# Shorter recurrence on TensorE, and two sequences' pages copied during the first layer

## What is computed

```python
for layer in range(2):                       # layer 0 is even, layer 1 is odd
    y = _even_mixer(x, ...) if layer == 0 else _odd_mixer(x, ...)
    x = _layernorm(ALPHA * x + y, ...)
    x = _layernorm(ALPHA * x + _moe(x, ...), ...)

# _odd_mixer: two mixers side by side, concatenated, one output projection
# C: RWKV-7, per head of 64, token by token:
    sa = einsum('bhvk,bhk->bhv', S, kk_t)
    S = S * w_t - sa[..., None] * (kk_t * a_t) + v_t[..., None] * k_t
    y_t = einsum('bhvk,bhk->bhv', S, r_t)
# D: latent attention; the sample group also reads 16 cached pages per sequence,
#    found through page_table (8 sequences x 16 pages)

# _moe: one router, 16 SwiGLU experts, each row goes to two of them
    he = silu(h @ w_gate[e]) * (h @ w_up[e]);  y += gate * (he @ w_down[e])
```

## Time and profile before

| | us |
|---|---|
| median of 3 runs | 1127.14 |
| lowest, highest | 1124.95, 1130.03 |
| the profiled execution | 1126.0 |
| its span, first to last instruction | 1124.2 |
| mean granted TensorE clock | 0.954 |

### The profile page before, as it was taken

One profiled execution on the slowest core, in us unless ns is written; L12 is line 12 of the kernel. 1 busy time (PEld: TensorE's weight loads), 2 busy tenths in 40 slices (PEclk: granted clock), 3 DMA queues, 4 the chain that ended last, 5 costly groups with the idle time before them and its releaser, 6 DMA issues.

```text
span 1124.2 us, 26894 instructions
## 1 busy us (share of the span) xinstructions
PE 1011.9 (90%) x11002; PEld 658.2 (59%) x11002; DVE 501.6 (45%) x1261; ACT 329.7 (29%) x889; POOL 129.8 (12%) x152
## 2 busy tenths in 40 slices
PE   9999996699998599999887789999999938999995
PEld 3687454466664367777666677655655525666641
DVE  1581134322222636497645663876523352222217
ACT  0102114133333224223333333264421132333321
POOL 0010000210000300000222220411000011100013
PEclk9999998699999799999899999899999968999997
DMA  9752205999996632122322224494443098999935
GB/s 316 300 86 75 98 38 210 335 348 371 379 409 227 206 150 76 38 91 74 92 78 72 78 77 141 135 366 169 170 177 150 26 349 270 381 369 371 402 118 203
DMA packets 80867, 225.41 MB, mean 201 GB/s; under 512 B 9424, under 2 KB 50432, under 8 KB 62432
## 3 DMA queue, kind: packets, MB, share of 16 engines
q1 hardware_dynamic: 65184, 153.29, 37.5%
q0 software_dynamic: 11968, 57.71, 15.5%
q10 hardware_dynamic: 3584, 12.58, 3.0%
HBM read 201.57 MB, written 40.86 MB: 216 GB/s over the span
## 4 chain that ended last, share of the span: by engine, by line
PE 83%; DVE 5%; DMA 5%; issue 4%; ACT 2%; POOL 0%; DVEq 0%; POOLq 0%; SPq 0%; ACTq 0%
PE bank L1367 16%; PE bank L1271 10%; PE bank L1558 9%; PE bank L1391 8%; PE bank L1466 6%; PE bank L1492 3%; PE bank L1660 3%; PE bank L1349 2%; PE bank L1529 2%; DMA work<-xkept,idx 1%; DMA xkept<-x 1%; PE bank L1971 1%; PE bank L1996 1%; PE bank L1282 1%; DMA work<-yrows,rowi 1%
## 5 line engine op out<-in xcount | busy, mean ns | idle before, releaser
L1271 PE MATMUL bank<-ring,cat 128*128 128x512 f32 x256 | 112.6, 594 | 1.3 <-ACT cat L2163 1.3
L1558 PE MATMUL bank<-xT,ring 128*128 128x288 f32 x448 | 110.9, 407 | 0.0
L1558 PEld LDWEIGHTS bank<-xT,ring 128*128 128x128 f32 x448 | 84.6, 190 | 23.8 <-issue 1.1
L1367 PE MATMUL bank<-ring,work 128*32 128x128 f32 (+1 forms) x1344 | 83.0, 318 | 1.7 <-DVE work L2620 1.7
L2630 DVE TENSOR_TENSOR work<-work,bank 128x192 f32<-128x192 f32 x32 | 11.3, 354 | 157.0 <-ACT work L2123 157.0
L1271 PEld LDWEIGHTS bank<-ring,cat 128*128 128x128 f32 x256 | 47.5, 190 | 57.2 <-issue 57.2
L2639 DVE COPY work<-bank 64x512 f32<-64x512 f32 x64 | 44.0, 688 | 67.2 <-PE bank L1391 66.7
L1367 PEld LDWEIGHTS bank<-ring,work 128*32 128x32 f32 (+1 forms) x1344 | 58.1, 122 | 25.1 <-issue 13.1
L1466 PE MATMUL bank<-xT,ring 128*128 128x288 f32 x256 | 63.1, 407 | 0.0
L2123 ACT ACTIVATE work<-bank 128x192 f32<-128x192 f32 x32 | 10.6, 331 | 163.0 <-PE bank L1367 163.0
L1466 PEld LDWEIGHTS bank<-xT,ring 128*128 128x128 f32 x256 | 48.3, 190 | 13.5 <-issue 0.4
(11 more groups left out here) (491 smaller groups left out, 1896.5 us busy)
## 6 DMA issues: line engine op xcount, KB each, us to landing
ring<-in_stream_dram SPq DMA_DIRECT2D x61, 1024.0 KB, 10.0
work<-in_stream_dram SPq DMA_DIRECT2D x16, 1024.0 KB, 16.7
cat<-in_stream_dram SPq DMA_DIRECT2D x16, 1024.0 KB, 19.0
by_batch<-in_pages_dram SPq DMA_DIRECT2D x128, 128.0 KB, 2.3
x<-in_stream_dram SPq DMA_DIRECT2D x12, 1024.0 KB, 18.6
xT<-in_stream_dram SPq DMA_DIRECT2D x12, 1024.0 KB, 16.9
yrows<-work ACTq DMA_DIRECT2D x32, 384.0 KB, 7.7
lnp<-in_ln_dram POOLq DMA_DIRECT2D x4, 1024.0 KB, 15.2
```

The costliest lines, as they stand in the source:

```text
L1271: i = pe.matmul(bank(n)[0:ROWS[tile], :], cat[:, k, tok(tile)], slot(w[k // 4], 4, 512)[:, k % 4, :], start=(k == 0), stop=(k == KC - 1))
L1367: i = pe.matmul(by_half[rows * q:rows * q + rows, :, to:to + width], xgT[:, e % 2, k, at:at + rows], w[:, :, width * q:width * q + width], ...
L1558: i = pe.matmul(bank(n + s)[:, 0:nn], slot(w, KC, 256)[:, k, P * (m % 2):P * (m % 2) + P], xT[:, k, a:a + nn], start=(k == 0), stop=(k == ...
```

## The change

In the recurrence of the prompt's tiles: `tokV`, `tokB` and `tokK` are each turned by four whole transposes into one bank instead of 32 instructions into two, and ScalarE evicts each with three instructions (one of 128 partitions, two of 64 that swap partition halves) instead of two. `N4` and `X1`, which both have `M2` as the stationary operand, become one piece `NX` whose moving operand is twice as wide; ScalarE copies both halves of `N4`, and VectorE adds `X0` to the other part to form `X1`, so GpSimd no longer forms `I + M2` but one half of `X0` in another layout. `NX` stands behind `M4`. Several waits that repeat an earlier one are dropped on TensorE. The sample tile only has its counts of `x0_ready` adapted.

On SyncE the pages of sequences 0 and 1 are copied in the first layer's experts branch, and those of sequences 2 to 7 where all were copied. GpSimd loads `table` near the start of the program instead of behind the first layer.

```diff
-            + halves(t, "tokV") + [("tokA", t, 0)] + before("S0") + halves(t, "N4") + before("yS") + halves(t, "M4")
-            + before("mean", "S1", "square") + halves(t, "X1", "M8") + before("var") + halves(t, "X2")
-            + before("inv0", "inv1") + halves(t, "G2V", "tokK", "X3") + before("inv2", "inv3") + halves(t, "Y")
-            + before("scale", "gate") + halves(t, "tokB", "HT", "H") + after("bA") + halves(t, "H2T") + after("M")
+            + [("tokV", t, 0), ("tokA", t, 0)] + before("S0") + halves(t, "M4") + before("yS") + halves(t, "NX")
+            + before("mean", "S1", "square") + halves(t, "M8") + before("var") + halves(t, "X2")
+            + before("inv0", "inv1") + halves(t, "G2V") + [("tokK", t, 0)] + halves(t, "X3") + before("inv2", "inv3") + halves(t, "Y")
+            + before("scale", "gate") + [("tokB", t, 0)] + halves(t, "HT", "H") + after("bA") + halves(t, "H2T") + after("M")
...
+EARLY_BATCHES = 2
...
+            def bring_together(b):
+                for i in range(NPG):
+                    page = sp.value_load(table[0:1, b * NPG + i:b * NPG + i + 1], min_val=0, max_val=A["pages"].shape[0] - 1)
+                    sp.dma_start(by_batch[b, :, :, P * i:P * i + P],
+                                 A["pages"][bass.ds(page, 1), :, :].rearrange("o p (w n) -> (o p) w n", w=2))\
+                        .then_inc(batch_gathered[b], 16)
...
                 if key == ("scratch", 0):
...
+                    for b in range(EARLY_BATCHES, DEC_B):
+                        bring_together(b)
...
                     layer = key[1]
                     rest = range(n, FIRST_EXPERT_BLOCK[layer] + 3 * N_EXP)
+                    if layer == 0:
+                        sp.wait_ge(table_loaded, 16)
+                        for b in range(EARLY_BATCHES):
+                            bring_together(b)
                     take(sp, job(f"{layer}.o{NT - 1}"))
                     for j in AHEAD[2:4]:
                         load_spare(layer, j)
...
+                        landed(pool, rec("M", tile, 1), 1)
+                        pool.tensor_tensor(d["XB"][:, 1], one, d["Nd"][:, 1], ALU.subtract).then_inc(x0_ready, 1)
...
                         landed(pool, rec("M4", tile, 0), 2)
+                        landed(pool, rec("NX", tile, 0), 2)
                         pool.tensor_tensor(d["I+M4"], both, d["M4"], ALU.add).then_inc(folded, 1)
...
+                                if name == "NX":
+                                    i = pe.matmul(bank(n + s, 4, 2, HD)[chunks[k ^ s], j], stays, NX[chunks[k], :, s, j, :],
+                                                  start=True, stop=True)
...
-                        if name != "tokK":
+                        if prompt or name != "tokK":
                             i = pe.transpose(bank(n, 4, P)[0:r, j, :], src[:, j, tok(tile)], ident)
...
+                if prompt and name == "NX":
+                    take(act, n)
+                    act.copy(d["N4"][:, half], bank(n, 4, 2, HD)[:, :, 0]).then_inc(n4_copied, 1)
...
+                    src, dst, sign = bank(n, 4, 2, HD), d[name[3]], -1.0 if name == "tokB" else 1.0
+                    act.activation(dst[:, 0], src[:, :, 0], ACT.Copy, scale=sign)
+                    act.activation(dst[0:CH, 1], src[CH:P, :, 1], ACT.Copy, scale=sign)
+                    give(act.activation(dst[CH:P, 1], src[0:CH, :, 1], ACT.Copy, scale=sign), n)
...
+                elif prompt and name == "NX":
+                    take(dve, n)
+                    dve.wait_ge(x0_ready, 3 * tile + 3)
+                    dve.wait_ge(n4_copied, 2 * tile + half + 1)
+                    give(dve.tensor_tensor(d["X1"][:, half], d["XB" if half == 1 else "XA"][:, half], bank(n, 4, 2, HD)[:, :, 1],
+                                           ALU.add), n)
```

More of the change, by code:

```diff
@@ L156 @@
 PAIRED = ("bA", "M", "kA", "EQ", "UV")
-CHAIN = ("N2", "M2", "N4", "M4", "X1", "M8", "X2", "X3", "Y", "HT", "H", "H2T", "Z", "TT", "G2V")
-TURNED = ("tokV", "tokB", "tokK")
-BY_ACT = ("N2", "M2", "X1", "Y", "HT", "Z", "G2V")
-BY_BOTH = ("N4", "M4", "X2", "X3", "TT")
+CHAIN = ("N2", "M2", "M4", "NX", "M8", "X2", "X3", "Y", "HT", "H", "H2T", "Z", "TT", "G2V")
+BY_ACT = ("N2", "M2", "Y", "HT", "Z", "G2V")
+BY_BOTH = ("M4", "X2", "X3", "TT")
 OFF_PE = ("square", "inv0", "inv1", "inv2", "inv3", "scale", "select")
@@ L1155, in recurrence @@
                             landed(pool, rec(name, LAST, 0), 2)
-                        landed(pool, rec("tokV", LAST, 0), 2)
+                        landed(pool, rec("tokV", LAST), 1)
                         landed(pool, rec("tokA", LAST), 1)
@@ L1195, in _ @@
             pool.dma_start(even, A["even"]).then_inc(even_loaded, 16)
+            pool.dma_start(table[:, :], A["table"]).then_inc(table_loaded, 16)
             pool.wait_ge(cleared, 1)
@@ L1611, in recurrence @@
                 at = lambda k: slice(P * tile + CH * k, P * tile + CH * k + CH)
-                if half > 0 and (name in PAIRED or prompt and (name in CHAIN or name in TURNED or name == "UW")):
+                if half > 0 and (name in PAIRED or prompt and (name in CHAIN or name == "UW")):
                     return
@@ L1676, in recurrence @@
                                 done(i, n + s)
-                elif prompt and name in TURNED:
-                    if name != "tokV":
-                        pe.wait_ge(decayed, 2 * tile + (1 if name == "tokB" else 2))
-                    src = {"tokV": V_, "tokB": beta, "tokK": kappa}[name]
-                    for s in range(2):
-                        claim(pe, n + s)
-                    for j in range(4):
-                        for s, k in four:
-                            i = pe.matmul(bank(n + s, 4, HD)[chunks[k ^ s], j], src[rows[s], j, at(k)],
-                                          c("ident64")[rows[s], :], start=True, stop=True)
-                            if j == 3 and k == 1:
-                                done(i, n + s)
                 elif prompt and name == "EQ":
                     landed(pe, rec("UW", tile, 0), 2)
-                    landed(pe, rec("bA", tile, 0), 2)
-                    landed(pe, rec("tokB", tile, 0), 2)
+                    landed(pe, rec("tokB", tile), 1)
                     for k in range(2):
@@ L1701, in recurrence @@
                 elif prompt and name == "UV":
-                    landed(pe, rec("UW", tile, 0), 2)
-                    landed(pe, rec("kA", tile, 0), 2)
-                    for other in TURNED:
-                        landed(pe, rec(other, tile, 0), 2)
+                    landed(pe, rec("tokK", tile), 1)
                     if tile > 0:
@@ L1740, in recurrence @@
                     if name == "X1":
-                        pe.wait_ge(x0_ready, 2 * tile + half + 1)
+                        pe.wait_ge(x0_ready, 3 * tile + half + 1)
                     if name == "G2V":
@@ L2262, in recurrence @@
                         give(act.copy(d["GV" if name == "G2V" else name][:, half], bank(n, 4, HD)), n)
-                elif prompt and name in TURNED:
+                elif prompt and name in ("tokV", "tokB", "tokK"):
                     take(act, n)
-                    give(act.activation(d[name[3]][:, half], bank(n, 4, HD), ACT.Copy, scale=(-1.0 if name == "tokB" else 1.0)), n)
+                    src, dst, sign = bank(n, 4, 2, HD), d[name[3]], -1.0 if name == "tokB" else 1.0
+                    act.activation(dst[:, 0], src[:, :, 0], ACT.Copy, scale=sign)
+                    act.activation(dst[0:CH, 1], src[CH:P, :, 1], ACT.Copy, scale=sign)
+                    give(act.activation(dst[CH:P, 1], src[0:CH, :, 1], ACT.Copy, scale=sign), n)
                 elif prompt and name == "UW":
@@ L2942, in recurrence @@
                     take(dve, n)
-                    dve.wait_ge(x0_ready, 2 * tile + half + 1)
+                    dve.wait_ge(x0_ready, 3 * tile + half + 1)
                     give(dve.tensor_tensor(d["XB"][0:r, half], d["XA"][0:r, half], src, ALU.add), n)
```

55 lines of the change are left out of this document (25 added, 30 removed).

## The result

The median of four runs went from 1127.56 us (1124.95 to 1130.03) to 1154.72 us (1149.77 to 1156.65), a ratio of 1.0234 with a 95% interval of 1.0202 to 1.0267: slower by 26.4 us of 1127.6. The profiled execution took 1156.65 us, its span is 1154.8 us and its mean granted clock 0.939.

The account below looks back on a forecast made before the run. TensorE sets the pace, with the weight stream barely keeping up in the first layer's experts. 1126.0 + 30.6 (late stream) + 1 (slower copy) - 2 (recurrence) = 1155.6, adjusted to the median and stated as 1156.5 us; range 1146 to 1168.

Parts of the forecast that it names:

- The place of the loop: First layer's experts, SyncE: the page copy starts at 184.3, behind the `ring` loads, not in the idle 70 us before.
- rival 1: Copy issued ahead of SyncE's wait for the output projection, so free: 1125 us, no slower; chance 0.04.
- The hold: First layer's experts: 32 page pairs hold SyncE 63.2 us; `cat` issued at 247.5, block 7 lands at 252.4.
- The slowdown by full DMA queues: Page copy in the first layer goes slower where DMA is full: 1 us taken, bounds 0 and 8.
- Rival 2: Page copy in the first layer costs only its bytes, 4.7 MB or 12 us: 1132 us; chance 0.05.
- The stream after the hole: First layer's experts: weight stream needs 127 us after block 7; last expert starts at 379.4, 30.6 us late, bounds 24.9 and 33.9.
- The clock: First layer's experts, TensorE's path: the first expert after the idle stretch runs slower, 1.7 us more.
- The pages out of the second layer: Second layer: SyncE's page loop gets 63 us shorter, hidden by the attention: 0 us, bounds -1 and 0.
- The recurrence: Prompt tiles: transposes, `NX` and fewer instructions against added ScalarE time; about -2 us in all, bounds -6 and +3.
- Half of what TensorE waits for in issue goes: Recurrence: the case behind its far bound of -6 us.
- rival 4: Recurrence gives back much: with all its "issue" waits gone (12 us) the total would be 1145; chance 0.05.
- The terms with a plus: Recurrence: ScalarE's evictions +0.33 us a tile ahead of `Y`, and +0.5 once in tile 0 for `M8` waiting on `NX`.

## Why the prediction was right, and where it was not

The time came out at 1154.7 us for 1156.5 predicted. That it slows down, and why, was foreseen; that the number fits so closely is luck, the sum of two misses that took each other back: the pages cost 40.3 us for 31.6, and the recurrence gave 10 to 15 for 2 in the totals (9.3 in the two profiles). Both lie outside the bounds that I had set for them, 33.9 for the stream (the up to 8 on top for a slower copy did not come) and -6 for the recurrence. A right total is no proof of its terms.

**The place of the loop: right.** It stood behind the `ring` loads, as the branch says; rival 1 was out. The version with the loop in the idle time shows that its mechanism was sound for another place of the loop: 63.9 us of issuing fit into the gap and cost nothing.

**The hold: right.** Predicted 32 pairs in 63.2 us from 184.3; it was 63.9 us from 185.03. `cat` issued at 248.94 (247.5) and landed 5.2 us later, at 254.1 (252.4). The slowdown by full DMA queues, taken as 1, does not show: the same 64 copies took 63.9 us in the idle gap too, where DMA has little to do. Rival 2, bytes alone, is out: the table above gives them no price beside the delay. What costs is SyncE's 1.93 us for a pair. The Trainium skill, "DMA: Bandwidth & Descriptors", section "Issuing engines are not separate DMA queues", calls the time to initiate a DMA usually small relative to the DMA itself. Here it is not: a pair is 0.15 MB, 0.4 us at the 385 GB/s of the earlier trace rows, and its two issues alone take 0.98 us.

**The stream after the hole: the step that failed.** I set the last expert at the later of two ends, TensorE's pace from the hole on and the stream's up to block 46. The stream itself was as fast as I thought. The tile view of `cat` for its last two blocks, 46 and 47 (first and last issue, then time to landing):

```profile
L972 SPq DMA_DIRECT2D cat<-in_stream_dram x2: 431/436/442, 360.6 to 361.1; - x2
...
DMA to landing us min/median/max: 23.3/24.3/25.3
```

If the shorter of the two times is that of the block issued first, block 46 landed at 360.6 + 23.3 = 383.9, 129.8 us after block 7, between my 127 and the slow bound of 130.3. But the last expert started at 388.3, 4.4 us later, and did not wait for it. The 14.5 us beyond TensorE's pace are 7.7 us of waits in the middle, at 288, 329, 339 and 350, and 6.8 us of slower products, nearly all behind the hole and two of the waits. Most of them come where row gathers and norm parameters share the DMA engines (373 and 376 GB/s in the windows), TensorE cannot win them back at 9.25 us an expert, and what the stream gains later, at 421 GB/s, arrives as unused lead. So the sum is: 1.8 us for the later landing of `cat`, 2.8 for the stream (129.8 - 127), 4.4 for a stream average in place of its worst stretch, 9 in all, which is 39.5 less 30.6; the 1 us taken for full queues covered a part. Put differently, a `cat` 63.2 us late was to cost 30.6, as if the stage had 33 us in hand; it had 20 to 25. The run with one sequence shows the same without any hole: 12.0 us late, from 11.3 us of waits in the middle and a slow clock behind one of them. Experts came every 10.3 us on average and not every 9.3 to 9.8, and the last at 388, not at 374 to 383.

**The clock.** 1.7 us were taken for TensorE's path, none on the stream's. Behind the hole the first products took 3.68 and 2.55 us for 1.95 and 1.90, 2.4 more, at a granted clock of 0.80 in that window, so partly at the lower of its two levels; behind the waits of 3.6 and 2.0 us 2.5 and 1.7 more; behind those of 1.3 and 0.8 us nothing. With the norm parameters moved, nothing was lost behind a wait of 2.0 us either (5.56 us).

**The pages out of the second layer: right.** Attention 150.3 us before, 151.8 after, 149.3 with the move alone.

**The recurrence: the mechanism named, the size wrong.** I had priced the transposes at -0.2, `NX` at -0.25 and fewer instructions at -0.4 us a tile, with +0.33 for ScalarE. The gain is uneven: the four tiles take 0.2 us more, and 5.3, 1.3 and 2.8 less, and in the first, where nothing is won, the clock was lower on both sides (0.90 before, 0.95 after). In the second tile (33.52 to 28.19) both run at full clock. TensorE's busy time gives 1.7 of its 5.3 us (25.34 to 23.60); I had 0.45. I read about 0.7 of it as the turnings and `NX`, and the other 1.0 as the last products that run out, 0.2 to 0.3 us each, ahead of five "issue" waits that are gone. That is argued, not tested. The rest of the 5.3 is idle time, 8.2 us before and 4.6 after. TensorE's waits in the change, beside the earlier trace rows (who for whom, total, times, longest):

```profile
PE bank L1675 <- ACT ring L2264: 4.1, 4, 1.0
PE bank L1672 <- ACT ring L2264: 4.1, 4, 1.0
PE bank L1675 <- DVE ring L2947: 4.0, 3, 1.3
PE bank L1675 <- issue: 3.9, 6, 1.4
```

"Issue" fell from 11.4 to 5.5 us over the four tiles, in the second from 5.6 to 0.6 us. From profile to profile it varies: 11.4 and 9.2 us in the two with the old recurrence, 3.8 to 7.3 (mean 5.1) in the seven with the new one. That is half, with 12.6% fewer instructions, so it does not go with their count, as I had assumed; with the turnings back, 3.5% fewer than before, it was 6.7. "Half of what TensorE waits for in issue goes" stood there as the far bound only. Of the 12 us of rival 4, then, half went.

The terms with a plus came too. The wait for ScalarE ahead of `Y`, four times, grew from 3.2 to 4.1 us in all (0.61 to 1.03 in two of the tiles): 0.9 for 1.3 foreseen. TensorE's waits for ScalarE as a whole went from 8.9 to 8.2 us. The waits for VectorE's copies of `H` came as foreseen (three times 1.33, 4.0 us), but those of `bA` for the gate that they replace were 1.4 us in all and not as much: this term was put at 0 and was +2.6. In the first tile `M8` waited 1.4 us for `NX`, where 0.5 was foreseen. So the gains of the recurrence were underrated by more than its total shows.

What stays open: why "issue" fell by half, and what else shortened the tiles. The split by edits is not settled, as said above; the copies beside it are ruled out as what makes the "issue" waits.

## What to carry to other kernels

Small transfers added to a queue cost here their issuer's time, not their bytes: look for the stretch in which that queue waits anyway, and put the work ahead of that wait. Where a stream and an engine run at nearly the same pace, compute the delay block by block with the bandwidth of the worst stretch, since here every wait in the middle was lost for good, and some had a slow clock behind them. A forecast that is made of a loss and a gain is tested only by running each part alone.

## What was not expected of the hardware

- "Issue" waits of TensorE in code of small products. In the recurrence of the kernel before there are 20, of 0.2 to 1.7 us. 15 of them, with 10.0 of the 11.4 us, lie 244 to 250 products and weight loads apart, or a multiple of that. The row for instruction loads of the change in the recurrence (queue, packets, MB, share):

```profile
q8 instruction: 26, 0.43, 1.5%
```

  That is 16.5 KB a packet, 26 of them while 6441 products and weight loads ran, one for 248; before had 30 packets for 7370, one for 246 (other engines' code may be among them). So the spacing of the waits is close to that of the loads of code. The Trainium skill, "Runtime: NRT & Kernel Launch", section "Instruction fetch mechanics", says that instructions are refilled in blocks of 16 KiB and that crossing a block is mostly hidden. The size agrees with the rows. That these waits are the block's crossing is an inference from the spacing; no run changed it alone. If they are, it is not hidden in such code: they add up to 11.4 us of 127.8.
- Two copies of 1 MB in rows of 512 bytes held SyncE for 11.4 us, and four of 64 KB for 10.8; the same for the other sequence took 2.9 and 5.1. That the long ones met full queues is a guess, and no run tests it.
- With the same code the recurrence took from 116.6 to 122.2 us in seven profiles, with granted clocks of 0.90 to 1.00 in single tiles; differences of 2 us in that stage need more than one profile.
